# A two-layer mixer and expert trunk: mLSTM state terms a step ahead, three barriers fewer in each layer, another order of weight units

## The reference

```python
for l in range(2):
    h_l = modulate(rmsnorm(x, g[0]), mod_l[0], mod_l[1])      # mod_* = silu(c) @ ada_w[l] + ada_b[l]
    h_c = modulate(rmsnorm(ctx, g[0]), mod_c[0], mod_c[1])
    qm, km, vm, om, gm, pu, qn, kn, vn, bg = split(h @ w_in[l])
    m = sigmoid(om) * head_rms(scan_forward + scan_backward)  # mLSTM, chunks of 128 tokens, 4 heads
    p = pool_branch(pu); n = na_latent(qn, kn, vn)            # pooling; neighbourhood attention
    y = (sum over branches of sigmoid(bg) * (branch @ w_branch[l])) @ w_out[l]
    x = x + mod_l[2] * rmsnorm(y, g[1])
    x = x + mod_l[5] * rmsnorm(ec_moe(h2, ...), g[3])         # each expert takes its top tokens

def step(carry, inp):                                         # one chunk of the mLSTM scan
    g = b + m[..., None]; mt = jnp.maximum(g, dmat.max(-1))
    sc = einsum('bhtd,bhsd->bhts', qc, kc) * exp(dmat - mt)
    inter = exp(g - mt)
    num = inter * einsum('bhvd,bhtd->bhtv', C, qc) + einsum('bhts,bhsv->bhtv', sc, vc)
    den = inter * einsum('bhd,bhtd->bht', n, qc) + sc.sum(-1)
    h = num / maximum(abs(den), exp(-mt))
    C_new = decay * C + einsum('bhs,bhsv,bhsd->bhvd', ws, vc, kc)
```

## Time and profile before

| | |
|---|---|
| median of 3 runs | 2785.39 us (2783.75 to 2786.51) |
| the profiled execution | 2786.34 us, of which the span from first to last instruction is 2784.6 us |
| mean granted clock of PE | 0.942 |
| PE busy | 2431.1 us (87% of the span) |
| DVE, ACT, POOL busy | 729.7, 616.1, 551.8 us |
| HBM read and written | 574.5 and 21.1 MB |
| chain that ended last | PE 47%, DMA 36%, issue 6%, DVE 5%, ACT 3% |

### The profile page before, as it was taken

One profiled execution on the slowest core, in us unless ns is written; L12 is line 12 of the kernel. 1 busy time (PEld: TensorE's weight loads), 2 busy tenths in 40 slices (PEclk: granted clock), 3 DMA queues, 4 the chain that ended last, 5 costly groups with the idle time before them and its releaser, 6 DMA issues.

```text
span 2784.6 us, 38818 instructions
## 1 busy us (share of the span) xinstructions
PE 2431.1 (87%) x16038; PEld 1540.2 (55%) x16038; DVE 729.7 (26%) x1401; ACT 616.1 (22%) x1038; POOL 551.8 (20%) x304
## 2 busy tenths in 40 slices
PE   3987979899999399999997597997899859988886
PEld 2766867788874244444443475776688433333332
DVE  3245035301001511111111426135210142322224
ACT  3233234322111211111111423233321121101011
POOL 1232231324420011111111223231455000000000
PEclk7999999999999699999998798999999979999998
DMA  6261331122140599999999245332223369999996
GB/s 225 88 232 61 121 99 35 46 68 68 48 156 0 207 347 387 389 391 391 390 390 362 89 150 194 82 99 72 68 91 99 109 268 403 410 411 403 408 409 263
DMA packets 177524, 593.92 MB, mean 213 GB/s; under 512 B 13928, under 2 KB 55280, under 8 KB 165040
## 3 DMA queue, kind: packets, MB, share of 16 engines
q1 hardware_dynamic: 164080, 561.18, 53.9%
q0 software_dynamic: 10304, 25.99, 3.4%
q10 hardware_dynamic: 3040, 5.31, 0.6%
HBM read 574.53 MB, written 21.05 MB: 214 GB/s over the span
## 4 chain that ended last, share of the span: by engine, by line
PE 47%; DMA 36%; issue 6%; DVE 5%; ACT 3%; SPq 1%; POOLq 1%; POOL 1%; DVEq 0%; ACTq 0%
PE ps L418 15%; DMA ring_lo<-in_w_gate 12%; DMA zone<-in_w_up 11%; DMA zone<-in_w_down 10%; PE ps L413 9%; PE ps L760 6%; PE ps L778 5%; PE ps L836 2%; PE ps L427 2%; PE ps L693 1%; DMA ring_lo<-in_ada_w 1%; PE ps L710 1%; POOLq L335 1%; PE ps L598 1%; DVE zone L1413 1%
## 5 line engine op out<-in xcount | busy, mean ns | idle before, releaser
L418 PE MATMUL ps<-hi_r,ring_r 128*128 128x512 f32 (+1 forms) x1792 | 477.0, 355 | 18.2 <-POOLq L335 14.8
L836 PE MATMUL ps<-ring_lo,zone 128*32 128x256 f32 (+1 forms) x3072 | 440.4, 494 | 31.1 <-DMA ring_lo<-in_w_gate 26.9
L418 PEld LDWEIGHTS ps<-hi_r,ring_r 128*128 128x128 f32 x1792 | 318.6, 191 | 67.1 <-POOLq L335 16.1
L1682 POOL TENSOR_TENSOR ring_r<-ring_lo,ring_r 128x2048 fp32r<-128x2048 f32 x52 | 239.6, 4610 | 482.2 <-ACT ring_r L929 481.8
L836 PEld LDWEIGHTS ps<-ring_lo,zone 128*32 128x32 f32 (+1 forms) x3072 | 156.9, 124 | 307.9 <-issue 280.3
L418 PE MATMUL ps<-lo_r,ring_r 128*128 128x512 f32 (+1 forms) x896 | 316.7, 353 | 0.0
L846 PE MATMUL ps<-zone 128*64 128x512 f32 (+1 forms) x2048 | 290.9, 495 | 0.9
L413 PE MATMUL ps<-ring_r,hi_r 128*128 128x512 f32 x736 | 234.5, 400 | 21.8 <-DVEq L335 21.8
L1787 POOL DMA_INDIRECT zone<-xn_dram,zone x36 | 40.5, 1124 | 860.0 <-DVE zone L1654 773.4
L846 PEld LDWEIGHTS ps<-zone 128*64 128x64 f32 (+1 forms) x2048 | 110.9, 125 | 164.0 <-issue 143.7
L418 PEld LDWEIGHTS ps<-lo_r,ring_r 128*128 128x128 f32 x896 | 170.7, 190 | 23.5
(11 more groups left out here) (272 smaller groups left out, 2584.7 us busy)
## 6 DMA issues: line engine op xcount, KB each, us to landing
ring_lo<-in_w_gate SPq DMA_DIRECT2D x64, 2048.0 KB, 10.9
zone<-in_w_down SPq DMA_DIRECT2D x64, 2048.0 KB, 10.1
ring_lo<-in_w_up SPq DMA_DIRECT2D x32, 2048.0 KB, 11.7
zone<-in_w_up SPq DMA_DIRECT2D x32, 2048.0 KB, 11.6
ring_lo<-in_w_in SPq DMA_DIRECT2D x52, 1024.0 KB, 5.3
ring_lo<-in_ada_w SPq DMA_DIRECT2D x24, 2048.0 KB, 11.7
ring_lo<-in_w_branch SPq DMA_DIRECT2D x24, 512.0 KB, 6.3
zone<-v_dram SPq DMA_DIRECT2D x128, 64.0 KB, 2.0
```

Of the source, the lines that this page charges most:

```text
L418: i = mm(dst[:, t0:t0 + tw], b[:, kk, f * P:(f + 1) * P], a[:, k, t0:t0 + tw], start=start and n == 0, stop=stop and n == 2)
L836: i = mm(bank(((2, 4), (3, 5))[s // 2][gi])[j * M:(j + 1) * M, 0:W], xeT[:, k, c0:c0 + M], w[:, k % 4, j * W:(j + 1) * W], start=(k == 0), ...
L1682: G.tensor_tensor(unit_lo(slot, ring_r), unit_lo(slot), unit_hi(slot, ring_r).bitcast(F32), ALU.subtract)\
```

## The change

On PE the state terms of step n+1 follow the products of step n, the products have banks 0 and 1 for themselves, and the conditioning units sit in fixed steps (`ADA_STEP`) with bank 7. ACT's scaled copy has two buffers. The barriers behind phases 3, 4 and 5 are gone (nine are left in a layer); semaphores of single steps stand in their place. The masks of three steps and the decays of two are made before the last v copy. The squares of the head sums move from DVE to ACT, into the scan, and DVE's two multiplications of a tile become four instructions. The transposes of the last head tile come between kn's first two features. The order of units and their slots is a table (`ORDER`), kn's second half is used first. Split 4 is done in step 8, on POOL in four pieces; splits 5 to 12 wait for the last `m_nd`, from 7 on for the last head rows; splits 13 and 14 stand at the beginning of the pooling stage. In the expert loop SP no longer waits for the load two before. The diff, cut to its core (PE, ACT, DVE, POOL and SP in this order):

```diff
-        qcs = cut(zone, 28976, "p (h n) -> p h n", 516, h=MH)
-        hsq = U[0]
+        qcs = [cut(zone, at_, "p (h n) -> p h n", 516, h=MH) for at_ in (28976, 27952)]
+        hsq = [cut(zone, at_, None, P) for at_ in (28468, 28596, 28724, 29492)]
...
+        ORDER = ((("ada", 0), 0), (("ada", 1), 1), (("ada", 2), 2), (("ada", 3), 0), (("qk", 0), 1), (("qk", 1), 2), (("v", 0), 0),
+                 (("v", 1), 1), (("ada", 4), 2), (("ada", 5), 0), (("ada", 6), 1), (("ada", 7), 2), (("ada", 8), 0), (("o", 0), 1),
+                 (("ada", 9), 2), (("ada", 10), 0), (("ada", 11), 2), (("o", 1), 0), (("kn", 1), 2), (("kn", 0), 1), (("qn", 0), 0),
+                 (("qn", 1), 2), (("vn", 0), 1), (("vn", 1), 0), (("pu", 0), 2), (("pu", 1), 0))
+        ADA_STEP = {0: 4, 1: 5, 2: 6, 4: 7, 5: 8, 7: 9, 8: 10, 10: 11}
+        O_BANKS = (6, 7, 0, 1, 2, 3)
+        KN_ORDER = ((3, 0, 1, 2), (1, 3, 0, 2))
...
+        HALVES = {"kn": (1, 0)}
...
-        NPH = 12
+        NPH = 9
...
-                phase_end(pe, ph + 3)
+                pe.wait_ge(sem("proj_out"), (l + 1) * PER["proj_out"])
...
+                def state_terms(n):
+                    st, r = n // 2, n % 2
+                    c = (FW, BWD)[r][st]
+                    u = outs.index((r, c))
+                    if st:
+                        pe.wait_ge(sem("m_C"), l * PER["m_C"] + n - 1)
+                    if u:
+                        pe.wait_ge(sem("m_qcs"), l * PER["m_qcs"] + u)
...
-                    if outp:
-                        pe.wait_ge(sem("m_sd"), l * PER["m_sd"] + u + 1)
-                        pe.wait_ge(sem("m_qcs"), l * PER["m_qcs"] + u + 1)
-                        for h in range(MH):
-                            i = mm(bank(2 + h % 2)[:, (h // 2) * 129:(h // 2) * 129 + 129], sdT[u % 2][:, h * P:(h + 1) * P], v_ext[:, c, h, :],
-                                   start=True, stop=True)
-                        i.then_inc(sem("m_num"), 1)
+                    if n in steps_out:
+                        u = outs.index((r, c))
                         if u + 1 < len(outs):
                             pair_scores(u + 1)
-                phase_end(pe, ph + 4)
+                        else:
+                            pe.wait_ge(sem("m_sd"), l * PER["m_sd"] + u + 1)
+                        if u:
+                            pe.wait_ge(sem("m_nd"), l * PER["m_nd"] + u)
+                        for h in range(MH):
+                            i = mm(bank(h % 2)[:, (h // 2) * 129:(h // 2) * 129 + 129], sdT[u % 2][:, h * P:(h + 1) * P],
+                                   v_ext[:, c, h, :], start=True, stop=True)
+                        i.then_inc(sem("m_num"), 1)
+                    if n + 1 in steps_out:
+                        state_terms(n + 1)
+                    if n in ADA_STEP:
+                        if ADA_STEP[n] == 8:
+                            pe.wait_ge(sem("ada_rows"), 3 * l + 2)
+                        ada_unit(l, ADA_STEP[n], 7)
...
-                head_cols(nt(l) - 1)
-                phase_end(pe, ph + 5)
...
+                def after_heads(n, f):
+                    if n == 1:
+                        head_cols(nt(l) - 1)
...
+                    if t in (2, 3):
+                        decays(t - 2)
...
+                    if n == 8:
+                        split(l, 4)
+                    if n >= 2:
+                        c = (FW, BWD)[n % 2][n // 2 - 1]
+                        if c < nt(l) and not first_visit(n % 2, c):
+                            squares(c)
+                ada_rows(l, 2, 7)
+                squares(summed[-2])
                 split(l, 5)
-                phase_end(act, ph + 4)
+                squares(summed[-1])
+                A_(hss[:, 0:4 * nt(l)], hss[:, 0:4 * nt(l)], ACT.Sqrt, bias=epsc, scale=1.0 / DV).then_inc(sem("hroot"), 1)
+                A_(amx, epsc, ACT.Sigmoid)
                 split(l, 6)
...
-                    if t == 1:
-                        split(l, 13)
...
-                phase_end(act, ph + 7)
-
+                phase_end(act, ph + 4)
+
+                split(l, 13)
+                split(l, 14)
...
-                split(l, 14)
-                phase_end(act, ph + 8)
+                phase_end(act, ph + 5)
...
+                decayed_scores(0)
...
+                        if u + 1 < len(outs):
+                            decayed_scores(u + 1)
                         dve.wait_ge(sem("m_num"), l * PER["m_num"] + u + 1)
+                        dve.wait_ge(sem("m_qcs"), l * PER["m_qcs"] + u + 1)
...
-                    link(V.tensor_tensor(hs, hs, hrr[:, 4 * t:4 * t + 4].unsqueeze(2).to_broadcast([P, MH, DV]), ALU.mult))
...
-                    V.tensor_tensor(hfin[t % 2], hsum[:, t, :], osig[t % 2], ALU.mult).then_inc(sem("hfin"), 1)
-                phase_end(dve, ph + 5)
+                    for h in range(MH):
+                        cols = slice(h * DV, (h + 1) * DV)
+                        i = V.scalar_tensor_tensor(hfin[t % 2][:, cols], hsum[:, t, cols], hrr[:, 4 * t + h:4 * t + h + 1],
+                                                   osig[t % 2][:, cols], ALU.mult, ALU.mult)
+                    i.then_inc(sem("hfin"), 1)
...
+                for u in range(3):
+                    masked(u)
+                pool.wait_ge(sem("proj_out"), (l + 1) * PER["proj_out"])
+                weighted(0)
...
+                    if n == 8:
+                        split(l, 4, 4)
+                pool.wait_ge(sem("m_nd"), l * PER["m_nd"] + len(outs))
+                for h in range(5, 13):
+                    if h == 7:
+                        pool.wait_ge(sem("hfin"), l * PER["hfin"] + nt(l))
                     split(l, h)
...
                         sp.wait_ge(sem("unit_done"), l * PER["unit_done"] + 6 * e + (s - 5))
                         sp.sem_inc(sem("sp_turn"), 1)
-
-                        s2, back = (s - 2) % 6, 1 if s < 2 else 0
-                        sp.wait_ge(w_ready(s2), 16 * e + 16 * (moe_base[l][s2] + 1 - back))
-                        sp.sem_inc(sem("sp_turn"), 1)
                         expert_unit(e, s)
```

More of the change, by code:

```diff
@@ L622, in _, with features @@
                             i.then_inc(sem("half"), 1)
-                head_cols(nt(l) - 1)
                 released[l, "o", 0] = ("half", l * PER["half"] + 3)
                 released[l, "o", 1] = ("oproj", l * PER["oproj"] + nt(l))
-                phase_end(pe, ph + 5)
-                def features(name, tag, g0, sts, free, order=range(KB)):
-                    for half in range(2):
+                def features(name, tag, g0, sts, bank_free, order):
+                    halves = HALVES.get(name, (0, 1))
+                    for x, half in enumerate(halves):
@@ new lines, in features @@
+                    released[l, name, halves[1]] = (tag, l * PER[tag] + g0 + KB)
+                def after_heads(n, f):
+                    if n == 1:
+                        head_cols(nt(l) - 1)
+                    if f == 2:
+                        pe.wait_ge(sem("mT"), l * PER["mT"] + nt(l))
+                    elif f == 1 and not first:
+                        pe.wait_ge(sem("m_qcs"), l * PER["m_qcs"] + len(outs))
+                    else:
+                        pe.wait_ge(sem("osig"), l * PER["osig"] + {3: 2, 0: 4, 1: 6}[f])
@@ L1672, in _, with split @@
             G = nc.gpsimd
[L1674 removed]
+            def split(l, h, parts=1):
                 slot = units[(l,) + SPLITS[h]][1]
```

287 lines of the change are left out of this document (139 added, 148 removed).

## The result

The changed kernel takes 2704.61 us (median of 4, 2699.11 to 2712.91), the kernel before 2785.95 in the same comparison (2783.75 to 2788.96). The ratio is 0.971, 95% interval 0.9683 to 0.9737: 81 us faster. The profiled execution has a span of 2702.2 us against 2784.6, 82.4 less.

What follows compares the result with a forecast made beforehand. PE was taken as bound by waits in the scan, at the seam to o and at pooling's end. Savings of 13.8 + 16.0 + 6.4 and 10.0 + 14.0 + 6.4, 66.6 us, gave 2719 from 2785.4; own range 2707 to 2732, chance 0.60.

Steps and rivals of the forecast that it cites:

- the expert loads gain: Rival: deeper queues even out the DMA engines, 15 us in layer 1, up to 4 in layer 0; 2700, chance 0.10.
- Steps with a unit: Scan steps with a conditioning unit on PE: PE's own work, 4.9 us each instead of 5.64.
- Steps without a unit: Scan steps without a conditioning unit: 3.0 us of PE work, bound by DVE at 3.4 to 3.9, taken as 4.2.
- The start of the scan: Layer 0: behind the last v copy only POOL's weighting precedes the first key-value product; first products end at 153.2.
- POOL's split in the scan: Split of o's first half, cut in four, in steps 9 and 10: 0 to 4.6 us of blocking, 3 taken.
- Layer 1's scan: Same count as in layer 0's scan: 10.0 us saved; loads come close and up to 4 may be lost.
- The seam in layer 1: Scan to o to kn: 14.0 us saved after 5 for DVE's late head rows; 19 if kn's split is earlier.
- The seam in layer 0: Scan to o to kn: idle 10.87, slow clock 2.4 and waits 3.1 go, 0.4 comes back; 16.0 us saved.
- Pooling: End of the pooling stage: PE's idle of 7.52 us shrinks to about 1.1, 6.4 saved in each layer.
- Expert loads: Expert loops without SP's wait: 0 taken; at most 1 us in layer 0, upper end 15 in layer 1.
- The rule against it: Shared port of DVE and POOL: cutting a split shortens each piece of blocking, not its sum; full blocking gives 2736.
- The rival, DVE held up by POOL's 2.3 us in every step: Rival: the scan keeps its pace, DVE needs 6.2 us a step, 17 us of the saving lost; 2736, chance 0.17.

Runs made afterwards that it cites:

- the one with the low parts first: The changed kernel with POOL's second gate-stage split and the two behind it held back until DVE has written the first branch's four low parts; 2689.98 us.
- the last kernel: On the one with the low parts first: layer 1's units in steps 3, 9, not 2, 8; ACT copies step 5's conditioning rows before decays; 2697.03 us.

## Why the prediction was right, and where its terms were off

2719 was forecast, 2704.6 measured, inside the range and faster as said. By its mechanism the likeliest case is the one that came: PE's waits in the scan, the idle at the seam and at the end of pooling went, and no run shows a gain from the loads. But the time lies 2.4 us below that case's own range (2707 to 2732) and is nearer to the 2700 of "the expert loads gain": the number alone would have pointed to the wrong case. And there is some luck in it: two parts gave 4.4 us less than forecast, the others 20 more. Of the parts:

- **Steps with a unit**: 4.9 forecast, 4.86 measured. The mechanism as put was "the one must be copied out before the other comes in", with the separate banks as cure. The runs show a second, sufficient cure that the prediction listed nowhere: the scores between state terms and products. And the state terms' place cures nothing.
- **Steps without a unit**: the term that was mis-sized in layer 0. I took them as bound by DVE at 4.2 us; the three took 2.97, 3.59 and 3.81, the last two with waits of 0.55 for POOL and 1.36 for DVE in them, so that PE's own work was all that was left. DVE did need 3.5 (from one state update, 165.59, to the next, 169.09), but PE didn't have to keep to it: with banks and buffers of their own a DVE that is half a microsecond late catches up in the next step with a unit, where it waits 0.77 us for PE (at 174.90). A bound holds only over as many steps as the buffers can't bridge. Without waits the three steps gave 4.1 us; waits of 4.25 in all (0.62 and 0.83 for ACT, 0.55 for POOL, 0.89 for a load, 1.36 for DVE) took the place of the 3 us of blocking that I had put in; with 0.2 from the start that makes the 3.1 by which layer 0's scan beat the forecast.
- **The start of the scan**: its terms add up to 152.9, where the prediction says 153.2. The first products ended 3.6 us behind the last v copy; the sum as written gives 3.7, its terms 3.4.
- **POOL's split in the scan** cost 1.36 us of wait, between the 0 and 4.6 given. With the split behind the scan it was 8 us a layer.
- **Layer 1's scan**: 8.6 instead of 10.0. "Loads come close" was right: waits of 2.64 and 1.73 us, and the units behind them in part at half clock (3.14 and 3.24 us instead of 1.95). With the products behind these units that is 7.6 us, more than the up to 4 allowed; that only 1.4 of it shows is due to what the sum had too high elsewhere, the steps without a unit and the blocking (6.2 us together).
- **The seam in layer 1**: the largest miss, 14.0 against 20.0. The stall of 5 us on DVE's head rows didn't come; the prediction had given 19 for that case. The term that was off is the time of ACT's split of kn's first unit, "about +14" behind the last product. ACT, POOL, DVE and PE there (the last product ended at 1663.20):

```profile
1670.69 1.90 ACT L961 ACTIVATE ring_r<-ring_lo 128x2048 fp32r<-128x2048 f32 x1
...
1672.66 4.60 POOL L1731 TENSOR_TENSOR ring_r<-ring_lo,ring_r 128x2048 fp32r<-128x2048 f32 x1 [1.10 <-ACT ring_r L961]
...
1677.57 1.14 DVE L1475 SCALAR_TENSOR_TENSOR zone<-zone,small 128x128 f32<-128x128 f32 x4 [8.02 <-ACT zone L1098]
...
1679.39 0.60 PE L623 MATMUL ps<-cst,zone 128*128 128x128 f32 x4
```

ACT split at +7.5, since its two table loads and the root took only 3 us and DVE's last four sums weren't blocked (1.14 us: POOL's split of o's second half waited for ACT until +3.8). POOL's split ended at +14.1, before ACT had the first sigmoid ready for DVE, and PE found the head rows written at +16.2.
- **The seam in layer 0**: 18.1 instead of 16.0. PE's work in the window fell from 38.87 us to 35.00; 0.6 of that are the last tile's transposes, which now stand between kn's features, so the slow clock had cost 3.3 us and not the 2.4 of the sum.
- **Behind the seam in layer 1**: 1.6 us that no term had. Before, kn's first products ran at half clock behind PE's last wait (1.22 us for two, at 1755.02); now they take 0.71.
- **Pooling**: 12.8 forecast, 11.5 measured, 3.4 in layer 0 and 8.1 in layer 1; of these, 0.5 and 2.1 lie in the attention ahead of the pooling stage, which no term covered, so that pooling itself gave 9.0. The term of 6.4 was right as far as PE's idle goes (7.52 became 1.01, 7.31 became 0.80), and "DVE's low parts of the branch keep their distance from the barrier, so I count nothing" was not enough: the distance stayed, 11.5 us, and with it DVE stayed the bound: before, the gate products ran at half clock while PE would have had to wait for DVE in any case; now they run at full speed, PE waits instead, and the half clock falls on the branch products, where nothing hides it.
- **Expert loads**: 0 forecast; the two runs on that wait show none.
- **The rule against it**: The Trainium skill, SBUF — State Buffer (on the shared port pair), says that the loser waits out the whole instruction. In the trace the four sums each ended 0.15 us behind one POOL instruction, which agrees. From the rule I had drawn that cutting shortens only the pieces: 5.27 us beside short pieces and 5.40 beside one bear that out. The rival, DVE held up by POOL's 2.3 us in every step, did not come, and the reason is one of timing: of DVE's 59 instructions of layer 0's scan without an operand in PSUM only 14 met POOL at all, and 11 of these were stretched, up to POOL's end; 27 with a PSUM operand met POOL, and none was. In step 4, for example, the first small operation took 0.83 us instead of 0.17, since it met POOL's weighting (DVE and POOL):

```profile
170.92 0.83 DVE L1456 SCALAR_TENSOR_TENSOR small<-zone 128x4 f32<-128x4 f32 x1
...
170.67 1.06 POOL L1759 TENSOR_TENSOR zone<-zone,small 128x516 f32<-128x516 f32 x1
```

What stays open: the 3.7 us of layer 1's experts, which no run ties to an edit; whether deeper queues widen the scatter; and the part of the four pieces.

## What to carry to other kernels

A wait on a shared buffer has more than one cure: before separating banks, see which independent work of the same engine can stand between the two uses; and separate them when a third engine's lateness should be bridged. The next wait after an edit is often the same pair of engines a stage later: here POOL's splits blocked DVE's low parts just behind the stage whose end they had left, and holding back the splits that nobody needs yet was worth 10.5 us in that stage. And price an idle of PE with the slow stretch behind it: 8.3 us of wait cost 11.

## What was not expected of the hardware

The clock's fall behind a wait of PE doesn't follow from the length of the wait alone. The same conditioning unit in layer 1, behind the same wait of 2.66 us for its load, kept full speed in the kernel with the order of the state terms undone (the first row; all 64 products at the usual pace, 1.95 us) and ran mostly at 1.2 GHz in the one with the low parts first (the second row, 3.61 us for 64):

```profile
1623.19 1.95 PE L431 MATMUL ps<-ring_lo,small 128*32 128x128 f32 x64 [2.66 <-DMA ring_lo<-in_ada_w]
...
1620.87 3.61 PE L431 MATMUL ps<-ring_lo,small 128*32 128x128 f32 x64 [2.66 <-DMA ring_lo<-in_ada_w]
```

Behind a wait of 1.73 us the clock fell in the changed kernel (a unit took 3.24 us), behind 1.72 in the kernel that waits for o's splits it did not, nor behind 2.06 in the last kernel. Behind every wait of 2.94 us or more that is shown here, the next products ran at 1.2 GHz. The price of a fall was about the same for short and long waits: 3 us in the changed kernel's first 10 us of branch products at a mean of 0.70, behind a wait of 2.94, and 2.7 in layer 0 of the kernel that waits for o's splits, behind 8.30.
